# Opening of a two-layer trunk kernel: one idle product fewer, and the first p load split over two issuing engines

## The reference, cut to what matters

```python
for i in range(DEPTH):
    h = _rmsnorm(x, pre_norm_g[i])
    z = h @ w_in[i]
    ...
    y = jnp.concatenate([oa * jax.nn.silu(ga), ob * jax.nn.silu(gb)], axis=-1) @ w_out[i]
    x = x + _rmsnorm(y, post_norm_g[i])
    gate = jax.nn.sigmoid(x @ w_ple_gate[i])
    e = (p[i] @ w_ple_proj[i]) * gate
    x = x + _rmsnorm(e, ple_norm_g[i])
```

## Time and profile before

| | |
|---|---|
| median of 3 runs | 356.63 us (356.52 to 356.67) |
| profiled execution, its own time | 357.37 us |
| span of the profiled execution | 355.5 us |
| PE busy | 347.4 us, 98% of the span |
| DVE, ACT, POOL busy | 262.8, 229.4, 68.3 us |
| mean granted PE clock | 0.997 |
| moved by the transfers | 61.12 MB, mean 172 GB/s |

### The profile page before, as it was taken

One profiled execution on the slowest core, in us unless ns is written; L12 is line 12 of the kernel. 1 busy time (PEld: TensorE's weight loads), 2 busy tenths in 40 slices (PEclk: granted clock), 3 DMA queues, 4 the chain that ended last, 5 costly groups with the idle time before them and its releaser, 6 DMA issues.

```text
span 355.5 us, 5701 instructions
## 1 busy us (share of the span) xinstructions
PE 347.4 (98%) x1927; PEld 291.4 (82%) x1927; DVE 262.8 (74%) x562; ACT 229.4 (65%) x459; POOL 68.3 (19%) x121
## 2 busy tenths in 40 slices
PE   8999999999999999999999999999999999999992
PEld 7797888888888888888888888888888888888882
DVE  2886979988865676786697587998897458678543
ACT  3897566776577955555667565788666796365221
POOL 1066640142200000003105624014220000000000
PEclk9999999999999999999999999999999999999998
DMA  7996797562753464658575927536356345650011
GB/s 266 380 358 205 66 319 241 170 183 63 201 186 130 136 196 158 207 164 156 181 232 146 353 85 207 165 114 189 113 156 198 120 133 186 214 172 8 2 50 68
DMA packets 31820, 61.12 MB, mean 172 GB/s; under 512 B 2376, under 2 KB 4432, under 8 KB 31792
## 3 DMA queue, kind: packets, MB, share of 16 engines
q1 hardware_dynamic: 30656, 57.48, 50.2%
q0 software_dynamic: 1120, 3.28, 5.1%
q10 hardware_dynamic: 16, 0.00, 0.0%
HBM read 59.71 MB, written 1.05 MB: 171 GB/s over the span
## 4 chain that ended last, share of the span: by engine, by line
PE 92%; DMA 3%; issue 2%; SPq 1%; ACT 1%; DVE 0%; POOLq 0%; DVEq 0%; POOL 0%
PE proj L1256 25%; PE proj L1258 25%; PE proj L1257 25%; DMA raw<-in_w_in_dram 3%; PE sc L1337 3%; PE tr L1407 2%; PE tr L1355 2%; PE pv L1424 2%; PE sc L1189 1%; PE pv L1429 1%; PE proj L1189 1%; PE proj L1200 1%; PE pv L1189 1%; PE proj L1162 1%; PE proj L1173 1%
## 5 line engine op out<-in xcount | busy, mean ns | idle before, releaser
L1256 PE MATMUL proj<-w_hi,act_hi 128*128 128x512 f32 (+1 forms) x392 | 157.0, 401 | 0.0
L1258 PE MATMUL proj<-w_hi,act_lo 128*128 128x512 f32 (+1 forms) x392 | 152.2, 388 | 0.0
L1257 PE MATMUL proj<-w_lo,act_hi 128*128 128x512 f32 (+1 forms) x392 | 151.6, 387 | 0.0
L854 DVE TENSOR_TENSOR w_lo<-raw,w_hi 128x1024 fp32r<-128x1024 f32 (+1 forms) x102 | 121.2, 1207 | 13.8 <-ACT w_hi L612 13.2
L612 ACT ACTIVATE w_hi<-raw 128x1024 fp32r<-128x1024 f32 (+2 forms) x103 | 102.6, 1023 | 4.5 <-DMA raw<-in_w_ple_proj_dram 2.6
L1258 PEld LDWEIGHTS proj<-w_hi,act_lo 128*128 128x128 f32 x392 | 73.6, 188 | 15.5
L1256 PEld LDWEIGHTS proj<-w_hi,act_hi 128*128 128x128 f32 x392 | 73.7, 188 | 14.1 <-issue 0.7
L1257 PEld LDWEIGHTS proj<-w_lo,act_hi 128*128 128x128 f32 x392 | 73.8, 188 | 12.9
L552 POOL TENSOR_TENSOR rstd<-var,minus_half 128x1 f32<-128x1 f32 x12 | 7.7, 641 | 190.5 <-DVE var L842 161.3
L748 ACT ACTIVATE probs<-probs,neg_max 128x128 f32<-128x128 f32 (+1 forms) x64 | 28.2, 443 | 5.2 <-DVE neg_max L1005 5.2
L542 POOL TENSOR_TENSOR v_all<-work,rot_tab 128x128 f32<-128x128 f32 x16 | 10.6, 665 | 75.7 <-ACT work L612 75.5
(11 more groups left out here) (225 smaller groups left out, 454.8 us busy)
## 6 DMA issues: line engine op xcount, KB each, us to landing
raw<-in_w_in_dram SPq DMA_DIRECT2D x59, 512.0 KB, 4.2
raw<-in_w_out_dram SPq DMA_DIRECT2D x16, 512.0 KB, 3.4
raw<-in_w_ple_gate_dram SPq DMA_DIRECT2D x16, 512.0 KB, 3.5
raw<-in_w_in_dram SPq DMA_DIRECT2D x7, 324.0 KB, 5.9
raw<-in_w_ple_proj_dram SPq DMA_DIRECT2D x4, 512.0 KB, 3.6
resid<-in_x_dram SPq DMA_DIRECT2D x2, 512.0 KB, 8.1
probs<-in_w_in_dram SPq DMA_DIRECT2D x2, 512.0 KB, 9.3
g_ple<-in_ple_norm_g_dram POOLq DMA_DIRECT2D x2, 512.0 KB, 4.9
```

What stands on the lines that cost most here:

```text
L854: nc.vector.tensor_tensor(w_lo[:, g % SLOTS, 0:nk * cols], landing(g, nk * cols), w_hi[:, g % SLOTS, 0:nk * cols].bitcast(fp32), ALU.subtr ...
L1256: nc.tensor.matmul(ps, src_hi[:, b, k0 + k, :], hi, start=(first_u and k == 0), stop=False)
L1257: nc.tensor.matmul(ps, src_hi[:, b, k0 + k, :], lo, start=False, stop=False)
L1258: last = nc.tensor.matmul(ps, src_lo[:, b, k0 + k, :], hi, start=False, stop=last_k)
```

## The change

Three edits. PE runs four idle products, no longer five. SP's first transfer carries only rows 0-127 of layer 0's p, and rows 128-255 are issued by ACT, ahead of the norm weight, with a semaphore of their own. PE waits for both semaphores ahead of the transposes of p.

```diff
-WARM = 5
+WARM = 4
...
+        p_late_in = sem("p_late_in")
...
-            sp.dma_start(p_raw[:, :, :], p[0, 0].rearrange("(q j) d -> q j d", j=2)).then_inc(p_in[0], 16)
+            sp.dma_start(p_raw[0:P // 2, :, :], p[0, 0, 0:P, :].rearrange("(q j) d -> q j d", j=2))\
+                .then_inc(p_in[0], 16)
...
+            act.dma_start(p_raw[P // 2:P, :, :], p[0, 0, P:2 * P, :].rearrange("(q j) d -> q j d", j=2))\
+                .then_inc(p_late_in, 16)
             act.dma_start(g8[:, :], pre_norm_g[0, :].rearrange("(k p) -> k p", p=P)).then_inc(g8_in, 16)
...
                     pe.wait_ge(p_in[m], 16)
+                    if m == 0:
+                        pe.wait_ge(p_late_in, 16)
```

## The result

The change made the kernel slower: 359.00 us (median of 6 runs, 358.56 to 360.40) against 356.57 us (6 runs, 355.99 to 356.88), a ratio of 1.0072 with a 95% interval of 1.0058 to 1.0085. That is 2.4 us. The prediction forecast no change (356.6 us, range 356.1 to 357.5); a slowdown of this size lies outside its range.

What follows compares the result with a forecast made beforehand. PE's list bounds the kernel from 13.73 us, the opening ending on the transfer stream. Terms of 0 and -0.05 us (stream) summed to -0.05 us, carried to the median: 356.6 us, range 356.1 to 357.5.

Steps and rivals of the forecast that it cites:

- the norm weight behind p's second half on ACT: Opening, ACT's queue: norm weight lands at 3.6 to 3.9, p's transposes start 0.1 to 0.4 us late; value 0.
- the gap of 0.61 us: PE standing still from 8.69 to 9.30, awaiting the second `w_ple_proj` unit; earlier PE work may slip 0.61 us free.
- The bound of 4.14: Latest norm weight landing: 3.49 plus an issue 0.43 to 0.65 us later, giving 3.92 to 4.14.
- The bound, and that a shift passes one for one: PE is gapless from 13.73 us; any shift of that moment passes to the end one for one.
- p in two halves, 0 to 0.33 us sooner: Opening transfers: two halves issued side by side land p as a whole 0 to about 0.33 us earlier; value 0.
- SP's issue of half of p, 0.05 us less: SP's first issue: 64 partitions instead of 128 save 0 to 0.05 us of the stream, bounded at 0.37.
- The idle product, value 0: PE's opening: dropping one product of some 0.5 us frees PE at about 3.05 but does not move p; value 0.
- ACT's own list and the second wait on PE, value 0: ACT's table load and copy move up to 0.65 us, covered by 1.97; PE's second wait bounded by 0.04; both 0.
- Rival A: PE's opening: pause at 3.05 us delays the clock's rise; 357.5 for half the first-unit stretch, 358.9 for all; chance 20%.
- the signs of being wrong: Weight loads drop to 137 ns after 7 us; second-unit pause gone, PE late; or second `w_ple_proj` unit well before 8.5.
- Rival C: Norm weight lands too late for the gap to cover: 0.04 us, or 0.2, giving 356.7 to 356.8; chance 3%.
- Rival B: Opening stream comes earlier through SP's sooner issues and better-spread p: 356.3, or 356.0 at the gap's end; chance 13%.

## Why the prediction was wrong

**The step that failed.** It is the term for the norm weight behind p's second half on ACT: "I take 3.6 to 3.9", 4.14 at the latest, value 0. The term was mis-sized. The norm weight was usable at 4.96, and p was transposed 1.44 us late against 0.1 to 0.4. With the gap of 0.61 us, 0.83 of that comes through, which brings the time to the upper edge of the range; without the gap it makes 358.1, well outside. The second failure is that the clock was left out of the sum and stood only as a rival. An estimate from the medians and the 347.4 us gives both their size: the second unit starts at some 9.2 us before the change and 11.6 after; of the 2.4 us between, 1.45 are p's later start (3.68 to 5.13) and the remaining 1.0 is the longer stretch from there at the lower clock.

The bound of 4.14 assumed that the second transfer of a queue takes as long from its issue as the first had. Its issue took 1.00 us, not 0.59, and its packets moved, all but a few, between 4.0 and 4.4 us. The norm weight had been earlier than the 3.49 that the bound used, too: with one idle product PE could take it at 2.54, so its landing has moved by 2.4 us. Exchanging the two ACT transfers made half of p late in its place. Which property of the transfer is the cause is not shown: p alone and first on ACT needed 4.1 us, and the norm weight first on GpSimd 4.1 and 5.5, so going beside SP's running weight stream is a rival to standing second.

**The bound, and that a shift passes one for one.** Right, and better than was claimed: the time is 347.4 us plus the start of PE's second embedding unit, in kernels from 356.06 to 360.75 us.

**"This gap of 0.61 us is the figure on which the case turns."** Wrong, but not what carried the time out of the range: without the gap, 0.1 to 0.4 us of delay would have made 356.7 to 357.0. The gap, and the `w_in` transfer that closed the opening, belonged to one execution whose weights landed late. No later profile of the kernel before or of its variants with other numbers of idle products has a wait there. The cover that I had set against every late microsecond does not exist in them: a late start is paid in full unless the clock gives it back. The profiled run's 0.74 us above the median, which I carried over as an offset, was a sign of this.

**p in two halves, 0 to 0.33 us sooner.** Wrong: the later half landed at 3.95, 0.3 us after the whole p of the kernel before. It cost nothing here, since the norm weight came later still.

**SP's issue of half of p, 0.05 us less.** Wrong in sign: 0.57 us against 0.37, 0.2 us more. With both halves on SP the ratio is 1.0035. That the weights were issued 0.2 us later was not shown to matter in the changed kernel itself, where DVE rounded the first unit at 5.47, well before PE could use it.

**The idle product, value 0.** Right: 1.0007 (0.9994 to 1.0020) by itself, and the changed kernel is as slow with five as with four.

**ACT's own list and the second wait on PE, value 0.** Right: the table load moved from 1.37 to 2.38, and ACT's next work waited for p all the same.

**Rival A, the clock.** The mechanism was right and was given too small a chance, and two of the signs of being wrong were seen: the loads were still at 230 ns after 7 us, and the pause ahead of the second unit was gone. Its pause was put at up to 0.85 us; it was 1.83. The 20% rested on three runs that lay within 0.15 us. Later runs of the same kernel spread from 355.87 to 357.66, which was to be seen only with more runs. Its price for the whole stretch, 358.9, lies on the result by luck: it is 2.9 us of low clock less a gap of 0.61, with no late start in it. What was measured is made otherwise. Between the profiles of 356.48 and 359.55 us lie 3.1 us, of which 1.45 are the start of p (3.68 to 5.13) and 1.66 the stretch from there to the second unit (5.34 to 7.00). The medians differ by 2.4 us.

**Rival C, the norm weight too late for the gap.** This is what happened, in kind, beside rival A. It had 3% because the bound of 4.14 was trusted. Its 0.2 us do not follow from its own terms either: 0.33 and half of 0.65, less 0.61, is 0.04.

**The two together.** Each of the two is nearly harmless alone: a pause with nothing late costs 0.07% in the median (one idle product), a late start without a pause 0.08% to 0.23% (nine on the kernel before, ten on the changed one). The late start without a pause finds the clock up sooner behind it, and the shorter work pays part of the delay back: in the profiles the stretch from p to the second unit is 4.92 us with nine and 4.27 with ten, against 5.34 in the second profile of the kernel before. The late start with a pause pays twice, 0.72%. Not explained is why the pause alone costs so little in the median, where its slowest runs have the changed kernel's whole stretch of 7.0 us. The rule of the Trainium skill that was cited against the change ("TensorE: Matmul & The Clock Gate", Part 1, The HAM clock gate), that throttled is the default and sustained activity releases it, agrees with this: without a pause ahead of p (nine and ten idle products) the loads are at 137 ns before the first unit's products, with one they are at 230 ns in the changed kernel.

**Rival B, the stream.** It did not occur. The rule cited for it ("DMA: Bandwidth & Descriptors", Issuing engines are not separate DMA queues, in the Trainium skill) grants two issuing engines the time of initiating and no more. Here not even that was saved: each half took 0.57 us to issue, the whole 0.37.

What stays open: why the norm weight, second on ACT, is served only after 4 us while SP's second half of p is there by 4.0. The packets show that q10 all but stood still from 3.5 to 4.0 us (2 packets) while q1 was full, not what decided between them. Open too is why DVE had to wait for the first unit of `w_ple_proj` until 7.13 in one kernel and until 4.8 to 6.6 in others.

## What to carry to other kernels

A second transfer on a queue that so far held one small one is a change of its own: if the head of an engine's list waits for it, look for the packets' own time in the trace and don't extrapolate the first transfer's. Slack that a single profile shows at the start of a kernel, where transfers vary by a microsecond between executions, is not cover until a second profile has it. And a pause in the matrix engine's opening is cheap or dear by what comes behind it. Where the operand behind it is late, it pays to fill the pause: here ten idle products, which filled it whole, brought back some 0.5% with no slow group of runs, and eight, which left 0.2 to 0.5 us of it, did so in half of the runs; five brought nothing. Where nothing was late, five to seven idle products made no measurable difference.

## What the runs showed of the hardware

- One transfer of 64 partitions (128 KB) took SP 0.57 us to issue, one of 128 partitions (256 KB) from the same tensor 0.37.
- The second transfer on ACT's queue was usable 3.6 to 4.0 us after its issue began (4 KB: 1.35 to 4.96 in the changed kernel, 1.35 to 5.36 with eight idle products; 128 KB: 1.36 to 5.13); 4 KB as the first were usable after 1.8 (0.73 to 2.54, one idle product), 256 KB as the first landed after 4.1, all of this beside SP's transfers. SP's second took 2.7 (1.37 to 4.05). On GpSimd 4 KB took 4.1 and 5.5 us.
- With unchanged instructions the lower clock lasted until about 5.0 us in one execution, which had a pause of 0.17 us, and beyond 8.0 in another, with a pause of 0.52 (eight idle products); the stretch behind p was 2.1 us longer for it.
- With PE at work without a pause from 1.05 us, weight loads were at 137 ns by 5.2 us in the first profile of the kernel before and still at 230 ns at 6.7 us with nine idle products. The granted clock read 1.00 in the openings before and after, at either level of the durations.
